# Twenty chunks of expert weights loaded ahead of the expert stage in place of sixteen

## The chip, the core and the metric

The kernel runs on one core of a Trainium2 chip. The metric is the device time of one execution in microseconds (us); lower is better. The core has TensorE (PE in the rows; its weight loads are PEld), VectorE (DVE), ScalarE (ACT), GpSimd (POOL) and SyncE (SP). SP computes nothing here: it issues most of the DMA transfers, one after the other in program order, and waits on semaphores between them. In the rows the issuing of a DMA has the engine name SPq or ACTq.

## What is computed

One step of a one-layer hybrid decoder for 256 prompt tokens and 64 sample tokens (320 in all, width 1024, float32): a token mixer of two branches (a chunked state-space scan with 16 heads, and an S5 scan), cross-attention into 256 memory tokens for each request, and a hierarchical mixture of experts: 4 groups of 8 experts, one group per token and the best two experts in it. The part that the change is about:

```python
def hier_moe(x, w_rg, b_rg, w_re, b_re, w_gate, w_up, w_down):   # x: 320 x 1024
    t = x.reshape(-1, D_MODEL)
    g_prob = jax.nn.softmax((t @ w_rg) + b_rg, axis=-1)
    g_idx = jnp.argmax(g_prob, axis=-1)
    ...
    comb = ((g_w * jax.nn.one_hot(g_idx, MOE_GROUPS))[:, :, None] * e_w[:, None, :])
    out = jnp.zeros_like(t)
    for g in range(MOE_GROUPS):                                  # 4 groups, 8 experts each
        hg = jax.nn.silu(jnp.einsum('td,edf->tef', t, w_gate[g])) * jnp.einsum('td,edf->tef', t, w_up[g])
        out = out + jnp.einsum('tef,efd->td', hg * comb[:, g, :, None], w_down[g])
    return out
...
h = h + memory_attention(rms_norm(h, norm_mem_q_g), mem_k, mem_v, w_mem_q, w_mem_o)
h = h + hier_moe(rms_norm(h, norm_ffn_g), ...)                   # then the final rms_norm
```

Each of the 32 experts has three matrices of 1024 x 512 in float32 (2 MiB each), so the expert weights are 192 MiB, and each is read once.

## The kernel before

**Stages.** The engines run programs of their own, written out by hand, with semaphores between them. First come the projections, the two scans and the gates; then the memory attention, whose sample part goes through the 8 requests one by one (SP fetches keys and values of 1 MiB each); then the output projection `o` in four parts of 256 columns and three blocks of tokens; then the router; then the expert stage, a loop over passes. A pass gives every expert up to 32 tokens; how many passes are needed is computed from the router's result, and these inputs need one.

**Units.** The 32 experts are handled in 8 quadruples (`NQ`), four experts side by side on TensorE (`EX = 4`, matmuls of 128x32 weights, which are the tokens, against 512 columns of expert weights). A quadruple `i` has six units: `U0` and `U1` (gate matrix, two halves), `U2` and `U3` (up matrix), `E0` and `E1` (down matrix). A unit needs four chunks of 1 MiB, one per expert. There are 48 units and 192 chunks; `ORDER` gives the units in time: U0 to U3 of quadruple 0, then for each next one its U0 to U3 followed by E0 and E1 of the quadruple before. TensorE's lines are L1888 (`gate_up`) and L1904 (`down`). Between the units stand side jobs (`phase_extras`): `X{i}.0` and `X{i}.1` gather the tokens of quadruple i with the selection `sel` (L1937), after which ScalarE and VectorE scale them into `xs` (L1161, L2641); `W{i}` turns the weights of the selected tokens (`selw`) into `wT`; `T{i}` transposes the hidden values, which VectorE writes in `hidden` (L2649); `S{i}.k` scatters the outputs back (L1963).

**Chunks and their places.** SP issues the 192 chunks in order (`load_chunk`, L588 and L590). The 16 places `raw[m % 16]` are regions of the two large tensors `ring` and `work`. The first 16 chunks go out while attention, the output projection and the router still run, and `left(m)` waits for the last reader of the place: chunk 0 for the sample attention of request 6 (`ob_full`), chunk 2 for request 7, chunk 5 for the last request, chunks 7 and 9 for the splitting of the first two parts of `w_mem_o`, chunks 11 and 13 for the third and fourth part of the output projection. From chunk 16 on SP waits at each multiple of four for the unit that held these four places (`unit_done`). The chunks of a unit count on a semaphore `raw_in`, one for each of four lanes; TensorE waits on it before the unit. The last unit's chunks are loaded in two halves (L588, L595).

**Around the start of the pass.** VectorE makes `sel` for quadruple 0, then (L2671 on) `weigh(0)` (L2628), `select(1)` (L2585) and `experts_in(0)` (L2641). TensorE starts with X0.0, with a matmul whose result is not used (`filler`, L1925) in its middle and another behind it, then U0. The router reads the transposed features `tT`, which eight `ft` jobs fill, and `lgT` is raised when the eighth logits matmul (L1799) has ended; ScalarE then copies the logits (L1133). While the router's small steps run, TensorE repeats matmuls whose result is not used (`busy`, L1836).

**The end.** After the last units VectorE adds up the output (L2663), multiplies the last rows by the final gain (`weighted`, L2669), and computes the variance (L2708) from the sums of squares that ScalarE made; then come the root, the scaling and the output DMAs.

## Time and profile before

| | |
|---|---|
| median of 3 runs | 1153.23 us |
| lowest and highest | 1151.77 and 1154.62 us |
| span of the profiled execution | 1153.6 us |
| TensorE matmul busy | 1001.8 us (87%) |
| VectorE busy | 460.6 us (40%) |
| ScalarE busy | 304.9 us (26%) |
| read from HBM | 286.76 MB |
| share of the main DMA queue | 65.5% of 16 engines |

The page shows one execution. Its busy times say how long an engine had instructions in it. The second part of the page cuts the span into 40 equal slices of 28.84 us; the row GB/s says what the DMA engines moved in each, and PEclk the clock that TensorE was granted, as a share of 2.4 GHz. In the rows of the timeline an instruction stands with its start, its duration, its engine and line, what it writes and reads, how many were merged (x4), and in brackets how long its engine had been idle and what ended that.

### The profile page before, as it was taken

What the parts mean: (1) busy time and instruction counts of PE and PEld (TensorE: products, weight loads), DVE (VectorE), ACT (ScalarE), POOL (GpSimd) and SP (SyncE); (2) the same over time, 40 slices, a digit from 0 to 9 for tenths busy, and PEclk for the clock granted to TensorE, in tenths of its full rate; (3) what the DMA queues carried; (4) which work ended last, traced back from release to release, by engine and by line L of the source; (5) the groups of instructions that cost most, each with busy time, mean ns of one, the idle gap of its engine ahead of it and who ended that gap; (6) DMA issues with size and microseconds to landing.
All of it is one profiled execution on the core that took longest, in us unless ns stands there. A gap on an engine that the chain in (4) does not pass through costs nothing.

```text
span 1153.6 us, 15983 instructions
## 1 busy us (share of the span) xinstructions
PE 1001.8 (87%) x6675; PEld 668.9 (58%) x6675; DVE 460.6 (40%) x787; ACT 304.9 (26%) x609; POOL 52.6 (5%) x76
## 2 busy tenths in 40 slices
PE   6999999999999999999898999867677877677565
PEld 4787567986679999999876954313131323232121
DVE  5999946204667554555455330010101010201014
ACT  3142123225436434544343331000000000000002
POOL 1604100010110000000000000000000000000000
PEclk9999999998999999999999999889788788887888
DMA  9482524012636284523677539999999999999994
GB/s 267 115 238 74 182 74 146 1 62 65 189 98 243 101 303 146 197 105 114 234 278 304 222 112 410 421 422 420 421 421 421 421 421 422 422 421 422 421 417 152
DMA packets 92435, 297.70 MB, mean 258 GB/s; under 512 B 21053, under 2 KB 31001, under 8 KB 68172
## 3 DMA queue, kind: packets, MB, share of 16 engines
q1 hardware_dynamic: 89812, 288.81, 65.5%
q0 software_dynamic: 2112, 7.28, 1.9%
q8 instruction: 54, 0.88, 0.3%
q10 hardware_dynamic: 440, 0.59, 0.2%
q14 instruction: 17, 0.14, 0.0%
HBM read 286.76 MB, written 9.90 MB: 257 GB/s over the span
## 4 chain that ended last, share of the span: by engine, by line
PE 40%; DMA 18%; SPq 13%; DVE 3%; issue 1%; ACT 1%; DVEq 0%; ACTq 0%
SPq L590 11%; DMA work<-in_w_exp_gate_dram 5%; DMA ring<-in_w_exp_down_dram 5%; PE bank L1607 5%; PE bank L1608 4%; PE bank L1609 4%; PE bank L1888 4%; DMA work<-in_w_exp_down_dram 3%; PE bank L1238 3%; DMA ring<-in_w_exp_gate_dram 2%; DMA ring<-in_w_exp_up_dram 2%; PE bank L1618 2%; PE bank L1620 2%; PE bank L1619 2%; PE bank L1937 2%; PE bank L1533 2%
## 5 line engine op out<-in xcount | busy, mean ns | idle before, releaser
L1888 PE MATMUL bank<-ring,work 128*32 128x512 f32 x768 | 139.7, 698 | 29.0 <-DMA work<-in_w_exp_gate_dram 14.9
L1888 PE MATMUL bank<-work 128*32 128x512 f32 x256 | 109.0, 690 | 22.2 <-DMA ring<-in_w_exp_gate_dram 15.3
L1253 PE MATMUL bank<-work,ring 128*128 128x320 f32 (+1 forms) x480 | 125.6, 420 | 0.0
L1607 PE MATMUL bank<-ops,usplit 128*128 128x320 f32 x368 | 114.2, 310 | 1.1 <-DVE usplit L2343 1.1
L1608 PE MATMUL bank<-ops,usplit 128*128 128x320 f32 x368 | 114.0, 310 | 0.0
L1609 PE MATMUL bank<-ops,usplit 128*128 128x320 f32 x368 | 113.9, 310 | 0.0
L1253 PEld LDWEIGHTS bank<-work,ring 128*128 128x128 f32 x480 | 90.2, 190 | 30.7 <-issue 1.0
L1904 PE MATMUL bank<-ring,work 128*32 128x512 f32 x384 | 86.4, 839 | 24.5 <-DMA ring<-in_w_exp_down_dram 13.1
L2343 DVE TENSOR_TENSOR usplit<-ring,usplit 128x2048 fp32r<-128x2048 f32 x32 | 73.3, 2291 | 62.3 <-ACT usplit L952 62.3
L1904 PE MATMUL bank<-work 128*32 128x512 f32 x128 | 63.6, 827 | 35.6 <-DMA ring<-in_w_exp_down_dram 35.6
L1888 PEld LDWEIGHTS bank<-ring,work 128*32 128x32 f32 x768 | 33.5, 126 | 76.1 <-issue 63.1
L952 ACT ACTIVATE usplit<-ring 128x2048 fp32r<-128x2048 f32 x32 | 61.4, 1920 | 51.9 <-PE bank L1609 36.7
L2641 DVE TENSOR_TENSOR work<-bank,g 128x512 f32<-128x512 f32 x8 | 5.5, 690 | 173.8 <-PE bank L1937 173.8
L1607 PEld LDWEIGHTS bank<-ops,usplit 128*128 128x128 f32 x368 | 69.2, 188 | 1.6 <-issue 1.5
L1937 PE MATMUL bank<-work 128*128 128x128 f32 (+1 forms) x384 | 69.4, 310 | 0.2 <-DVE work L2585 0.2
L1608 PEld LDWEIGHTS bank<-ops,usplit 128*128 128x128 f32 x368 | 69.1, 188 | 0.1
L1609 PEld LDWEIGHTS bank<-ops,usplit 128*128 128x128 f32 x368 | 69.2, 188 | 0.0
L1937 PEld LDWEIGHTS bank<-work 128*128 128x128 f32 (+1 forms) x384 | 53.0, 190 | 27.5 <-issue 14.0
L1888 PEld LDWEIGHTS bank<-work 128*32 128x32 f32 x256 | 23.2, 124 | 66.4 <-issue 58.2
L2656 DVE COPY work<-bank 128x512 f32<-128x512 f32 x8 | 5.5, 692 | 136.3 <-PE bank L1904 136.3
L1618 PE MATMUL bank<-usplit,ops 128*128 128x256 f32 (+1 forms) x192 | 54.6, 284 | 1.7 <-DVE ops L2348 1.7
L1620 PE MATMUL bank<-usplit,ops 128*128 128x256 f32 (+1 forms) x192 | 53.9, 281 | 0.0
(449 smaller groups left out, 1527.6 us busy)
## 6 DMA issues: line engine op xcount, KB each, us to landing
ring<-in_w_exp_up_dram SPq DMA_DIRECT2D x50, 1024.0 KB, 25.9
ring<-in_w_exp_gate_dram SPq DMA_DIRECT2D x46, 1024.0 KB, 26.0
ring<-in_w_exp_down_dram SPq DMA_DIRECT2D x45, 1024.0 KB, 26.0
ring<-in_w_in_dram SPq DMA_DIRECT2D x11, 2048.0 KB, 9.1
work<-in_w_exp_gate_dram SPq DMA_DIRECT2D x18, 1024.0 KB, 25.6
work<-in_w_exp_down_dram SPq DMA_DIRECT2D x15, 1024.0 KB, 25.6
work<-in_w_exp_up_dram SPq DMA_DIRECT2D x14, 1024.0 KB, 25.7
ring<-in_w_glu_dram SPq DMA_DIRECT2D x4, 2048.0 KB, 8.1
```

The costliest lines, as they stand in the source:

```text
L590: sp.dma_start(raw[m % RAW], src).then_inc(raw_in[m // EX % (RAW // EX)], 16)
L952: act.activation(uhi[u % 2], unit_raw(u), ACT.Copy).then_inc(s["whi"], 1)
L1253: ins = nc.tensor.matmul(b[:, 0:N], wv[:, k, P * (m % 4):P * (m % 4 + 1)], src[:, k, 0:N], start=(k == 0), stop=(k == KT - 1))
L1607: nc.tensor.matmul(b[:, 0:T], wh, hi_[:, k], start=(k == 0), stop=False)
L1608: nc.tensor.matmul(b[:, 0:T], wh, lo_[:, k], start=False, stop=False)
L1609: ins = nc.tensor.matmul(b[:, 0:T], wl, hi_[:, k], start=False, stop=(k == KT - 1))
L1618: nc.tensor.matmul(b[0:R, 0:256], th_, uhi[u % 2][:, k], start=(k == 0), stop=False)
L1620: ins = nc.tensor.matmul(b[0:R, 0:256], tl_, uhi[u % 2][:, k], start=False, stop=(k == KT - 1))
L1888: ins = nc.tensor.matmul(psum[part][ES * x:ES * (x + 1), :], xs[i % 2][:, kk, x], wt[x][:, k], start=(kk == 0), stop=(kk == KT - 1))
L1904: ins = nc.tensor.matmul(psum[2 + n_][ES * x:ES * (x + 1), :], hhT[:, j, x], wd[x][:, k, BLK * n_:BLK * (n_ + 1)], start=(j == 0), stop=(j ...
L1937: ins = nc.tensor.matmul(b[:, P * j:P * (j + 1)], tn[0:R, c, 4 * r_ + j], sel[i % 2][0:R, c].rearrange("p x n -> p (x n)"), start=(c == 0) ...
L2343: TT(ulo[u % 2], unit_raw(u), uhi[u % 2].bitcast(F32), ALU.subtract).then_inc(s["wlo"], 1)
```

## The change

The number of chunks that are loaded before the first unit is done goes from 16 to 20 (`AHEAD`). The four new places are:

- `early`: a new tensor of 2092 columns, out of which small tensors of the token mixer (`lpow`, `slp`, `lam`, `wdt`, `dtb`, `alog`, `cst`, `last3`, `dsm`) are now cut. Its chunk waits for `hl1`, a job of the state-space scan that is over long before. It takes part in the rotation for the rest of the pass.
- `xs` (columns 4096 to 6143 of `work`): the later home of `xs[1]`, `sel[1]` and `selw`. Chunk 6 goes there once the last request's attention is done.
- `ysb` (columns 6656 to 8703): the later home of the hidden values and the output sums. Chunk 14.
- `wT` (columns 18688 to 20735): the later home of `wT`. Chunk 15, when the router's logits are there (`lgT`).

The last three are used once, by the first twenty chunks; after that 17 places rotate, so that chunk m waits for the unit of chunk m - 17. The order in which the first twenty are issued is `BEGIN`. The semaphores `raw_in` go from four lanes to six.

So that the lent places stay untouched until their unit has read them, some work moves: `tT` goes to another part of `work`, `plc` and the scratch of the squares too; the matmuls `busy` read `h` in place of `tT`; VectorE does `experts_in(0)` first, then waits for unit U1 of quadruple 0, and only then does `weigh(0)` and `select(1)`, which write into the place of chunk 6; in quadruple 0 TensorE does X1.0 after U2 (before: after U1) and X1.1 after U3 (before: after U2). At the end of a pass VectorE waits for its own `weighted` results (`hg`) before it goes on to the variance.

```diff
-RAW = 16
+AHEAD = 20
+LANES = 6
+HOME = (["early", 0, 1, 2] + [3, 4, "xs", 5] + [6, 7, 8, 9] + [10, 11, "ysb", "wT"] + [12, 13, 14, 15])
+LENT = ("xs", "ysb", "wT")
+BEGIN = [0, 1, 2, 3, 4, 5, 6, 14, 7, 8, 9, 10, 11, 12, 13, 16, 17, 18, 19, 15]
+def places():
+    place, before_it = list(HOME), [None] * AHEAD
+    kept = [m for m in range(AHEAD) if HOME[m] not in LENT]
+    for m in range(AHEAD, NCH):
+        p = kept.pop(0)
+        place.append(place[p])
+        before_it.append(p)
+        kept.append(m)
+    return place, before_it
+PLACE, HELD_BY = places()
...
-        x["U1"] = [f"X{i + 1}.0"]
-        x["U2"] = [f"X{i + 1}.1"]
+        x["U2" if i == 0 else "U1"] = [f"X{i + 1}.0"]
+        x.setdefault("U3" if i == 0 else "U2", []).insert(0, f"X{i + 1}.1")
...
-        lpow = sb("lpow", [P, 2, Q + 1, NST])
+        early = sb("early", [P, 2092])
+        lpow = of_early(2, Q + 1, NST)
...
-        tT = w(3072, KT, T)
+        tT = [w(18296 + T * k, T) for k in range(KT - 1)] + [w(8704, T)]
...
-        plc = w(19680, NC, NG * NE)
+        plc = w(9088, NC, NG * NE)
...
+        home = dict(enumerate(raw)) | {"early": early[:, 0:CH], "xs": work[:, 4096:4096 + CH], "ysb": work[:, 6656:6656 + CH],
+                                       "wT": work[:, 18688:18688 + CH]}
...
-                if m == 0:
+                at = PLACE[m]
+                if at == "early":
+                    got(sp, "hl1")
+                elif at == 0:
                     sp.wait_ge(s["ob_full"], NB - 2)
-                elif m == 2:
+                elif at == 2:
                     sp.wait_ge(s["ob_full"], NB - 1)
-                elif m == 5:
+                elif at == "xs":
                     sp.wait_ge(s["ob_full"], NB)
...
+                elif at == "wT":
+                    sp.wait_ge(s["lgT"], 1)
...
-                for m in range(NCH):
+                for m in BEGIN:
                     left(m)
-                    if m >= RAW and m % EX == 0:
-                        sp.wait_ge(s["unit_done"], rr * NU + ((m - RAW) // EX + 1))
+                    load_chunk(m)
+                for m in range(AHEAD, NCH):
+                    u = HELD_BY[m] // EX
+                    if m == AHEAD or u > HELD_BY[m - 1] // EX:
+                        sp.wait_ge(s["unit_done"], rr * NU + (u + 1))
                     load_chunk(m)
...
-                    nc.tensor.matmul(psum[7][:, :], ones[:, :], tT[:, 0:2].rearrange("p k t -> p (k t)")[:, 0:BLK], start=True, stop=True)
+                    nc.tensor.matmul(psum[7][:, :], ones[:, :], h[:, 0, 0:BLK], start=True, stop=True)
...
+                experts_in(0)
+                unit("U", 0, 1)
                 weigh(0)
                 select(1)
-                experts_in(0)
...
                     dve.wait_ge(s[f"got{b}"], (rr + 1) * USES[b])
+                dve.wait_ge(s["hg"], rr * 2 + 2)
                 dve.sem_inc(s["pass_done"], 1)
```

SP's queue at the start of the pass, before: the names are the destination and the source tensor; the row with ISA is the wait for the first unit.

```order
L615 ISA
L590 DMA work<-in_w_exp_gate_dram 128x2048 x2
L590 DMA ring<-in_w_exp_gate_dram 128x2048 x2
L590 DMA work<-in_w_exp_gate_dram 128x2048
L590 DMA ring<-in_w_exp_gate_dram 128x2048 x3
L590 DMA ring<-in_w_exp_up_dram 128x2048 x7
L590 DMA work<-in_w_exp_up_dram 128x2048
L620 ISA
```

The same place in the changed kernel:

```order
L654 ISA
L624 DMA early<-in_w_exp_gate_dram 128x2048
L624 DMA work<-in_w_exp_gate_dram 128x2048 x2
L624 DMA ring<-in_w_exp_gate_dram 128x2048 x2
L624 DMA work<-in_w_exp_gate_dram 128x2048 x2
L624 DMA work<-in_w_exp_up_dram 128x2048
L624 DMA ring<-in_w_exp_gate_dram 128x2048
L624 DMA ring<-in_w_exp_up_dram 128x2048 x6
L624 DMA ring<-in_w_exp_gate_dram 128x2048 x3
L624 DMA work<-in_w_exp_gate_dram 128x2048
L624 DMA work<-in_w_exp_up_dram 128x2048
L662 ISA
```

Twenty transfers now stand ahead of the wait for the first unit, the four more being chunks 16 to 19 of quadruple 1's gate matrices, and the last issued is chunk 15.

TensorE between the units of quadruple 0, before, from the end of U1 to the start of U3 (L1888 is a unit's matmuls, 16 in all, and L1937 a side job X of 12):

```order
L1888 MATMUL bank<-ring,work 32x512 x3
L1930 REGISTER_ALU
L1937 MATMUL bank<-work 128x128 x12
L1888 MATMUL bank<-ring,work 32x512 x16
L1937 MATMUL bank<-work 128x128 x12
L1888 MATMUL bank<-ring,work 32x512 x3
```

The same place in the changed kernel, up to the first matmuls of the next quadruple's U0 (L1929 for L1888, L1978 for L1937; L1280 are the side jobs W0, of three, and T0, of four):

```order
L1929 MATMUL bank<-ring,work 32x512 x17
L1971 REGISTER_ALU
L1978 MATMUL bank<-work 128x128 x12
L1929 MATMUL bank<-ring,work 32x512 x2
...
L1978 MATMUL bank<-work 128x128 x12
L1280 MATMUL bank<-ident,work 128x128 x2
L1280 MATMUL bank<-ident,work 128x64
L1280 MATMUL bank<-ident,work 128x128 x4
L1929 MATMUL bank<-ring,work 32x512 x3
```

The last matmul of U1 and the sixteen of U2 are now one row; X1.0 stands behind them, and X1.1 between U3 and W0.

VectorE at the start of the pass, before, with the semaphores waited for:

```order
L2628 TENSOR_TENSOR work<-work,comb 128x384 [waits sel]
L2585 TENSOR_TENSOR work<-ranks,work 128x384
L2609 ISA
L2641 TENSOR_TENSOR work<-bank,g 128x512 [waits side4]
L2641 TENSOR_TENSOR work<-bank,g 128x512 [waits side7]
L2616 ISA [waits sil]
L2649 TENSOR_TENSOR work<-bank,work 128x512 [waits unit_done]
```

And in the changed kernel:

```order
L2682 TENSOR_TENSOR work<-bank,g 128x512 [waits side4]
L2657 ISA
L2668 ISA [waits unit_done]
L2669 TENSOR_TENSOR work<-work,comb 128x384 [waits sel]
L2626 TENSOR_TENSOR work<-ranks,work 128x384
L2682 TENSOR_TENSOR work<-bank,g 128x512 [waits side7]
L2657 ISA [waits sil]
L2690 TENSOR_TENSOR work<-bank,work 128x512 [waits unit_done]
```

The scaling of X0.0 (L2641, now L2682) has moved ahead of `weigh(0)` and `select(1)`, and a wait for a unit stands between them.

## Rows read from the trace of the kernel before

**Rows 1.** The page: span, and what the DMA engines moved in 40 slices.

```profile
span 1153.6 us, 15983 instructions
...
GB/s 267 115 238 74 182 74 146 1 62 65 189 98 243 101 303 146 197 105 114 234 278 304 222 112 410 421 422 420 421 421 421 421 421 422 422 421 422 421 417 152
```

**Rows 2.** DMA view from 760 to 1100 us.

```profile
DMA packets 19645, 143.20 MB, mean 421 GB/s; under 512 B 2177, under 2 KB 2177, under 8 KB 2177
```

**Rows 3.** Chain of work that ended last, in order of time: start, duration, what.

```profile
1124.22 11.20 DMA work<-in_w_exp_down_dram
```

**Rows 4.** Timeline of SP's queue: start, duration, line, transfer, count.

```profile
606.73 0.37 SPq L509 DMA_DIRECT2D ring<-in_cache_mem_v_dram  x1
613.73 0.82 SPq L590 DMA_DIRECT2D work<-in_w_exp_gate_dram  x2
...
625.90 1.28 SPq L590 DMA_DIRECT2D ring<-in_w_exp_gate_dram  x3
...
649.29 6.12 SPq L590 DMA_DIRECT2D ring<-in_w_exp_up_dram  x4
...
668.79 0.43 SPq L590 DMA_DIRECT2D work<-in_w_exp_up_dram  x1
...
691.08 0.80 SPq L590 DMA_DIRECT2D work<-in_w_exp_gate_dram  x2
```

**Rows 5.** Windows: stretch, length, engines' busy time, PEclk, DMA share, GB/s.

```profile
610.00:614.00 4.00, 3.94 (x49) 2.98 (x51) 2.12 (x5) 1.63 (x5) 0.00 (x0) 1.00 0.29 118
...
640.00:644.00 4.00, 4.00 (x37) 4.00 (x36) 1.51 (x3) 0.00 (x0) 0.00 (x0) 1.00 0.02 10
...
677.00:678.00 1.00, 1.00 (x4) 0.23 (x3) 0.70 (x4) 1.00 (x1) 0.00 (x0) 1.00 0.14 57
...
680.00:684.00 4.00, 4.00 (x16) 2.49 (x15) 2.48 (x11) 1.05 (x1) 0.00 (x0) 0.72 0.00 0
...
692.00:693.00 1.00, 1.00 (x7) 0.81 (x6) 0.00 (x0) 0.00 (x0) 0.00 (x0) 1.00 1.04 205
693.00:694.00 1.00, 1.00 (x8) 0.82 (x6) 0.00 (x0) 0.00 (x0) 0.00 (x0) 1.00 0.85 319
```

**Rows 6.** Timeline from the router's logits to the end of the first unit.

```profile
671.57 0.43 ACT L1133 ACTIVATE work<-bank 36x320 f32<-36x320 f32 x1 [0.84 <-PE bank L1799]
...
681.75 2.07 PE L1925 MATMUL bank<-work,ones 128*128 128x512 f32 x2
...
682.41 0.55 DVE L2585 TENSOR_TENSOR work<-ranks,work 128x384 f32<-128x384 f32 x1
...
686.33 1.13 PE L1925 MATMUL bank<-work,ones 128*128 128x512 f32 x2
...
686.43 0.69 DVE L2641 TENSOR_TENSOR work<-bank,g 128x512 f32<-128x512 f32 x1 [3.47 <-PE bank L1937]
...
687.38 0.62 PE L1888 MATMUL bank<-work 128*32 128x512 f32 x2
...
690.95 4.30 PE L1937 MATMUL bank<-work 128*128 128x128 f32 x24
```

**Rows 7.** Timeline of units U1 to U3 of quadruple 0 and their side jobs.

```profile
700.05 4.30 PE L1937 MATMUL bank<-work 128*128 128x128 f32 x24
...
704.28 3.64 PE L1888 MATMUL bank<-ring,work 128*32 128x512 f32 x32
...
715.78 1.05 DVE L2649 TENSOR_TENSOR work<-bank,work 128x512 f32<-128x512 f32 x1 [2.91 <-PE bank L1888]
...
716.98 0.63 PE L1238 MATMUL bank<-ident,work 128*128 128x128 f32 x4 [0.70 <-DVE work L2649]
717.54 0.62 PE L1888 MATMUL bank<-work 128*32 128x512 f32 x2
```

**Rows 8.** Timeline of VectorE at the end.

```profile
1142.55 0.68 DVE L2669 TENSOR_TENSOR work<-work,s5p 64x512 f32<-64x512 f32 x1
1143.15 0.14 DVE L2708 SCALAR_TENSOR_TENSOR var<-ssp,var 128x3 f32<-128x3 f32 x1
```

More of the change, by code:

```diff
@@ L50 @@
 NCH = EX * NU
-assert NCH % RAW == 0
 LASTU = NU - 1
+AHEAD = 20
[3 more added lines that the diff above has]
+BEGIN = [0, 1, 2, 3, 4, 5, 6, 14, 7, 8, 9, 10, 11, 12, 13, 16, 17, 18, 19, 15]
+assert len(HOME) == AHEAD and NU % LANES == 0 and sorted(BEGIN) == list(range(AHEAD))
+def places():
[8 more added lines that the diff above has]
+PLACE, HELD_BY = places()
 def phase_extras(i):
@@ L262, in layer, with of_early @@
         sel16 = sb("sel16", [P, 4, 2])
-        lpow = sb("lpow", [P, 2, Q + 1, NST])
-        slp = sb("slp", [P, 2, NST])
+        early = sb("early", [P, 2092])
+        early_at = [0]
+        def of_early(*dims):
+            n = 1
+            for d in dims:
+                n *= d
+            at = early_at[0]
+            early_at[0] += n
+            return view(early[:, at:at + n], dims)
+        lpow = of_early(2, Q + 1, NST)
+        slp = of_early(2, NST)
         vec = sb("vec", [P, 124])
-        lam = sb("lam", [P, 104])
+        lam = of_early(104)
         hglu = sb("hglu", [P, KT])
@@ L270, in layer @@
         s5p = sb("s5p", [P, 16, NST])
-        wdt = sb("wdt", [P, KT, HEADS])
+        wdt = of_early(KT, HEADS)
         wr = sb("wr", [P, KT, NG + NG * NE])
         rbias = sb("rbias", [P, NG + NG * NE])
-        dtb = sb("dtb", [P, HEADS])
-        alog = sb("alog", [P, HEADS])
-        cst = sb("cst", [P, CT, 3 * NB])
-        last3 = sb("last3", [P, CT, 27])
+        dtb = of_early(HEADS)
+        alog = of_early(HEADS)
+        cst = of_early(CT, 3 * NB)
+        last3 = of_early(CT, 27)
         ss = sb("ss", [P, 5])
@@ L295, in layer @@
         w_in_sem = [sem(f"w_slot{i}") for i in range(STAT_SLOTS)]
-        raw_in = [sem(f"raw_in{i}") for i in range(RAW // EX)]
+        raw_in = [sem(f"raw_in{i}") for i in range(LANES)]
         def bank(job):
@@ L391, in layer @@
         ytmp = w(23300, 192)
-        dsm = sb("dsm", [P, 12, NC, HEADS])
+        dsm = of_early(12, NC, HEADS)
         dtx, dte, dtl, dtm, dt_, dtA, csk, tot, wend, etot = (dsm[:, i] for i in range(10))
@@ L1115, in features @@
                 got(act, f"ft{k}")
-                emptied(act.activation(tT[:, k], bank(f"ft{k}")[:, 0:T], ACT.Copy), f"ft{k}")
+                emptied(act.activation(tT[k], bank(f"ft{k}")[:, 0:T], ACT.Copy), f"ft{k}")
             for i in range(3):
@@ L1798, in logits @@
                     pe.wait_ge(s["osb"], NB)
-                ins = nc.tensor.matmul(psum[6][0:NG + NG * NE, 0:T], wr[:, k], tT[:, k], start=(k == 0), stop=(k == KT - 1))
+                ins = nc.tensor.matmul(psum[6][0:NG + NG * NE, 0:T], wr[:, k], tT[k], start=(k == 0), stop=(k == KT - 1))
                 if k == KT - 1:
@@ L1873, in loaded @@
                 def loaded(u):
-                    n_ = RAW // EX
-                    pe.wait_ge(raw_in[u % n_], (rr * (NU // n_) + (u // n_ + 1)) * (16 * EX))
-                    return [raw[m % RAW] for m in range(EX * u, EX * u + EX)]
+                    pe.wait_ge(raw_in[u % LANES], (rr * (NU // LANES) + (u // LANES + 1)) * (16 * EX))
+                    return [home[PLACE[m]] for m in range(EX * u, EX * u + EX)]
                 def gate_up(i, j):
@@ L2513, in features @@
                 got(dve, f"ft{k}")
-                emptied(dve.tensor_copy(tT[:, k], bank(f"ft{k}")[:, 0:T]), f"ft{k}")
+                emptied(dve.tensor_copy(tT[k], bank(f"ft{k}")[:, 0:T]), f"ft{k}")
             dve.memset(rtl, 0.0)
```

17 lines of the change are left out of this document (9 added, 8 removed).

## The prediction

> **What bounds the kernel now.** I read the slices of the page first. From the 25th slice (692 us) to the 39th the DMA engines move some 421 GB/s in every slice, and in the four slices before they move 234 to 304, then 222 and 112 [rows 1]. The DMA view of the stretch from 760 to 1100 us gives the level exactly: 421 GB/s without a dip [rows 2]. So the expert stage is a stream of weights at one rate, and TensorE follows it. The chain of waits agrees: its last long piece is the wait of 11.20 us for w_exp_down, up to 1135.42, and behind it come only the last matmuls and the tail [rows 3]. A stage of this kind ends at (start of the gapless stream) + (bytes still to come) / (rate) + (tail). Whatever makes TensorE faster in it is worth nothing; what counts is when the stream starts and how much it still has to carry.
>
> Then I read where the stream starts. SP has issued the sixteenth chunk at 668.79 and can issue the next only at 691.08, when the first unit is done and its four places are free [rows 4]. The transfers end at about 677 (57 GB/s in 677 to 678), then nothing moves for some 15 us (0 GB/s from 680 to 684), and data flows again between 692 and 694 [rows 5]. The reader is to see an idle resource right ahead of the stretch in which it is the bound. The 15 us have room for six chunks, but no place to put them.
>
> **The change part by part.**
>
> *Four chunks out of the stream.* A chunk is 1 MiB, 1.0486 MB; at 421 GB/s [rows 2] it takes 2.49 us. When the first unit is done, 192 - 20 = 172 chunks are to come in place of 176. If all twenty have landed by then, the stream ends 4 x 2.49 = 9.96 us sooner. This term is the forecast; the rest is whether its conditions hold.
>
> *Do the four more transfers fit in idle DMA time?* Chunk 0 now goes to the early tensor, whose wait is long over, so it is issued right behind the last value load at 606.73, at about 607.1, and not at 613.73 [rows 4]. The DMA engines are 29% busy from 610 to 614 [rows 5]. The value load stands ahead of it in the queue and is for the last request, whose attention ends only at about 625.9, where SP's next wait ends [rows 4]; even a delay by one full chunk, 2.49 us, leaves that cover. The chunks for the xs and ysb places go out at 625.9 with the four others there, six in place of four, 5 us more of transfer. The old four have ended by 640 (10 GB/s from 640 to 644 [rows 5]), and SP's next issue is at 649.29 [rows 4]. So 5 us more end at about 645, in the hole. At about 668 SP issues three chunks as before (now 17, 18 and 19 where it was 13, 14 and 15), which end at about 677. The last one, chunk 15, waits for the logits; ScalarE copies those at 671.57 [rows 6], so it is queued by 671.7 and lands at 677 + 2.5 = 679.7 at the latest rate. All twenty are there 11 us before the first unit ends, and no step on the path waits for them. Cost of the four on the path: nothing, and 2.49 us for each that would not have landed in time.
>
> *The start of the first unit.* On VectorE the scaling of X0.0 moves ahead of weigh(0) and select(1). Before, these two instructions of 128x384 (0.55 us each, one at 682.41) ended by 683, and VectorE then sat idle for 3.47 us until X0.0 was there at 686.43 [rows 6]. So nothing was late by them and nothing is won. On TensorE the order up to the first unit is the same, with busy reading another tensor of the same shape. The first unit starts at 687.38 and ends at 690.95, 3.57 us, and SP issues 0.13 us later [rows 4, 6]. I take this as unchanged, 0 us. A bound below nothing: TensorE's clock is at 0.72 from 680 to 684 [rows 5], and the unused pair of matmuls takes 2.07 us there against 1.13 us at 686.33 [rows 6]. If the granted clock stayed at 2.4 GHz there, some 2 us would be won; if it came back later, about as much lost. Neither is in the change.
>
> *The new wait of VectorE for U1.* Behind it in its queue stand weigh(0), select(1), the scaling of X1.1 and hidden(0). TensorE needs select(1) for X1.0, which now comes after U2. In times of before: U1 ends at 700.05, the two instructions of 0.55 us are through by about 701.3, and U2 runs to 703.6, so X1.0 finds its selection. That is why X1.0 was moved, and U2 covers the wait. Without U2 the cost would be 1.2 us of TensorE, and none of the stream.
>
> *The next thing that is late: unit U0 of quadruple 1.* The stream must not run dry. After the first unit SP may issue chunks 20 to 23, after U1 24 to 26, after U2 27 to 30, after U3 31 and 32: 13 chunks, and the 14th waits for the fifth unit. Before, 16 chunks could be issued by then. So I compute both ends. The stream: 421 - 205 plus 421 - 319 are missing in the two windows from 692 to 694 [rows 5], which is 0.76 us, so it starts in effect at 692.76, 1.68 us behind SP's issue at 691.08. Thirteen chunks of 2.49 us keep it fed until 725.1. The unit: with 3.57 us for a unit [rows 6] and 4.23 us for a side job X (700.05 to 704.28 [rows 7]), U2 ends at 703.6, X1.0 at 707.85, U3 at 711.4, X1.1 at 715.65. The scaling of X1.1 takes 0.69 us and some 0.1 us of signal, to 716.45. hidden(0) then needs 1.20 us until T0 starts (715.78 to 716.98), and the unit starts 0.56 us after T0 (717.54) [rows 7]: 718.2, where it was 717.54. It ends at 721.8, SP issues at 721.9, and the data flows from 723.6. That is 1.5 us before the stream would run dry. Cost: nothing as computed; if this unit is late by more than 1.5 us, each further microsecond is paid in full. From there on the stream is fed in time, since each unit and its side jobs take at most 3.6 + 4.2 us and a unit's four chunks take 9.96 us.
>
> *Seventeen places in rotation.* Chunk m waits for the unit of m - 17 where it was m - 16. Since the stream has no dip in rows 2, a deeper rotation has nothing to give, 0 us.
>
> *The wait for hg at the end.* The trace of before does not show it. The second product starts at 1142.55 and takes 0.68 us, and the variance starts at 1143.15 without waiting for its end at 1143.23 [rows 8]. With the wait it starts a little after 1143.23. The bounds are 0.08 us (the rest of the product) and 0.7 us (a whole instruction of that size); I take 0.12 us, near the first, as only a signal comes on top. It is on the path: nothing covers it.
>
> *The sum.* -9.96 + 0.12 = -9.84 us. Against the profiled execution: 1153.6 - 9.8 = 1143.8 us. The median of the runs shown is 0.4 us below this span, so for the median 1153.23 - 9.84 = 1143.4 us.
>
> *A rule against a row.* The rate of the stream carries the whole term, and the trace shows 421 GB/s [rows 2]. The Trainium skill, "DMA: Bandwidth & Descriptors", section "Where 436 GB/s comes from", says that for transfers from HBM to SBUF the HBM side binds at about 358 GB/s. By an estimate from that page's figure a chunk would take 2.93 us and four would give 11.7 us. The row is measured in this very stretch, so the measurement decides, and that outcome gets no chance of its own.
>
> **The rivals.**
>
> *A. The stream runs dry for a while, or a chunk lands late.* The 14th chunk waits for a unit with 1.5 us to spare, and this margin is worked out from sums of a dozen short steps. If the chain from U3 to the next quadruple takes 3 to 5 us more than computed (a side job that waits for a semaphore I took as ready), 1.5 to 3.5 us go. If one of the four chunks does not land in time, 2.49 us go. Against it: the wait for the logits ends at 671.6 and leaves 11 us. Time: 1145 to 1148.5, say 1146.5 us.
>
> *B. The change does not do what it says.* If the DMA engines slowed down by what the chunks save, for instance because the stream writes places that TensorE reads at the same time more than before, the time would stay. It takes a rate of 421 x 172/176 = 411 GB/s over the stream. Against it: the stream holds 421 GB/s in fifteen slices through all sixteen places and all phases of TensorE. Time: 1153 us.
>
> *C. Slower: TensorE's clock.* TensorE falls to 1.2 GHz around 680, after the thin matmuls of the router, and is back before the first unit. If in the new order it came back only after quadruple 0, the first unit would take 3.6 us more, U1 to U3, the three X jobs and the fifth unit together some 27 us more (about what they take now, 691 to 721.8, less the waits), so the stream would start 3.6 us late and then be dry for 27 + 3.6 - 3.6 - 1.5 = 25.5 us: 3.6 + 25.5 - 9.8 = 19 us slower, 1172 us. It decides once its loss passes 9.8 us: beyond the first unit (3.6 us) and the 1.5 us to spare, when the low level lasts through 9.8 - 3.6 + 1.5, about 8 us of TensorE's work as it is timed now. Against it: the granted clock is 1.00 in 692 to 694 [rows 5], and the changed order puts U1 and U2 back to back, with fewer gaps and not more. The Trainium skill, "TensorE: Matmul & The Clock Gate", section "What's actually happening", says that the throttled clock is the default and activity releases it; by that rule, too, the new order is no worse.
>
> **How the numbers follow.** Forecast 1143.4 us with 0.80; within it the spread of a median (the three runs lie 1.5 us to either side) and the clock's 2 us around the first unit give 1141 to 1146. Rival A 0.12, rival B 0.04, rival C 0.02, and 0.02 for anything else that is slower. The range takes the forecast's own and half of rival A: 1140.8 to 1147.0. A measurement of this kernel tells about 0.3%, 3.5 us, from no change, so faster means below 1149.8: the forecast and rival A, 0.92. Same: rival B, 0.04. Slower: 0.04.
>
> **What would show it.** In the profile of the changed kernel: SP issues 20 chunks before its first wait for a unit, the last at about 671.7; the DMA engines are idle from about 680 to 692; the first unit still ends at about 691; the windows from 692 to 730 show 421 GB/s throughout (a dip near 724 would be rival A); the last pieces land some 10 us sooner, at about 1125.5; from there to the end of the span it takes 18.1 us, as before, plus 0.1. The forecast is wrong if the first unit ends more than 2 us later, or the stream's rate is not 421, or the windows around 724 dip.

## The result and the profile after

| | before | changed |
|---|---|---|
| median of the comparison (4 runs each) | 1153.42 us | 1145.51 us |
| lowest and highest | 1151.77 and 1154.62 us | 1144.06 and 1147.27 us |
| ratio with its 95% interval | | 0.9928 (0.9916 to 0.994) |
| span of the profiled execution | 1153.6 us | 1141.9 us |

The changed kernel is 7 to 10 us faster; the forecast was 1143.4 us, 9.84 us faster. In the comparisons of the experiments before has 54 runs with a mean of 1153.55 us. The changed kernel has nine runs, four here and five in e1, with a mean of 1145.18 us and a median of 1144.71 us. The means differ by 8.4 us, with a standard error of 0.4.

SP's queue in the profile after (the rows that answer to [rows 4]): start, duration, line, transfer, count.

```profile
606.81 0.37 SPq L542 DMA_DIRECT2D ring<-in_cache_mem_v_dram  x1
607.53 0.96 SPq L624 DMA_DIRECT2D early<-in_w_exp_gate_dram  x1
...
668.86 0.43 SPq L624 DMA_DIRECT2D work<-in_w_exp_gate_dram  x1
671.63 0.33 SPq L624 DMA_DIRECT2D work<-in_w_exp_up_dram  x1
689.54 0.33 SPq L624 DMA_DIRECT2D early<-in_w_exp_gate_dram  x1
...
698.64 0.33 SPq L624 DMA_DIRECT2D ring<-in_w_exp_up_dram  x1
```

Chunk 0 goes out at 607.53, chunk 15 at 671.63 (the forecast said 671.7), and the first refill at 689.54, where it was 691.08.

Windows of the profile after, to be held against [rows 5]: stretch, length, busy times of PE, PEld, DVE, ACT and POOL, granted clock, DMA share, GB/s.

```profile
677.00:678.00 1.00, 1.00 (x4) 0.21 (x3) 0.75 (x5) 1.00 (x1) 0.00 (x0) 1.00 0.99 418
678.00:680.00 2.00, 1.77 (x14) 1.62 (x15) 1.04 (x4) 1.95 (x5) 0.00 (x0) 1.00 0.81 340
680.00:684.00 4.00, 4.00 (x22) 2.80 (x21) 1.51 (x9) 1.11 (x1) 0.00 (x0) 1.00 0.02 10
...
698.00:702.00 4.00, 4.00 (x41) 1.07 (x33) 1.03 (x2) 0.60 (x1) 0.00 (x0) 1.00 1.01 424
...
720.00:724.00 4.00, 4.00 (x40) 1.32 (x32) 0.00 (x0) 0.34 (x1) 0.00 (x0) 1.00 1.02 424
```

The transfers that ended at 677 now run to 680, all twenty chunks are there, and the stream has no dip at 700 or at 724. The granted clock from 680 to 684 is 1.00, where it was 0.72 [rows 5].

The end in the profile after: first the last long piece of the chain of waits, then VectorE's timeline (compare [rows 3, 8]).

```profile
1112.25 11.07 DMA work<-in_w_exp_down_dram
```

```profile
1130.45 0.68 DVE L2710 TENSOR_TENSOR work<-work,s5p 64x512 f32<-64x512 f32 x1
1131.37 0.16 DVE L2751 SCALAR_TENSOR_TENSOR var<-ssp,var 128x3 f32<-128x3 f32 x1 [0.24 <-DVE work L2710]
```

The last weights are there at 1123.3, 12.1 us sooner. The variance starts 0.92 us behind the start of the product, where it was 0.60.

### The profile page after: what moved, and what is told of

Read it like the earlier page. It is cut to its first block, busy times and chain, and to the rows that moved or that the text cites. A ratio compares the mean times of both kernels' runs of the same rounds, so it can differ in the third digit from the quotient of the medians.

```text
span 1141.9 us, 15982 instructions
## 1 busy us (share of the span) xinstructions
PE 993.6 (87%) x6675; PEld 666.6 (58%) x6675; DVE 460.7 (40%) x787; ACT 304.6 (27%) x609; POOL 52.7 (5%) x76
## 4 chain that ended last, share of the span: by engine, by line
PE 36%; SPq 32%; DVE 3%; DMA 2%; issue 2%; ACT 1%; DVEq 0%; ACTq 0%
SPq L624 30%; PE bank L1649 5%; PE bank L1650 5%; PE bank L1651 5%; PE bank L1280 3%; PE bank L1929 2%; PE bank L1978 2%; PE bank L1660 2%; PE bank L1662 2%; PE bank L1661 2%; PE bank L1575 2%; SPq L622 1%; PE bank L1620 1%; DMA ring<-in_state_ssd_dram 1%; DMA work<-in_w_exp_down_dram 1%
## 5 line engine op out<-in xcount | busy, mean ns | idle before, releaser
L1929 PE MATMUL bank<-ring,work 128*32 128x512 f32 x704 | 130.9, 680 | 37.2 <-DMA ring<-in_w_exp_gate_dram 19.4
L1945 PE MATMUL bank<-ring,work 128*32 128x512 f32 x352 | 74.2, 818 | 40.7 <-DMA ring<-in_w_exp_down_dram 30.0
L1929 PE MATMUL bank<-work 128*32 128x512 f32 x256 | 85.7, 689 | 14.1 <-DMA work<-in_w_exp_up_dram 6.8
L1929 PEld LDWEIGHTS bank<-ring,work 128*32 128x32 f32 x704 | 32.0, 123 | 100.0 <-issue 80.3
L2682 DVE TENSOR_TENSOR work<-bank,g 128x512 f32<-128x512 f32 x8 | 5.5, 692 | 162.5 <-PE bank L1978 162.5
L1978 PE MATMUL bank<-work 128*128 128x128 f32 (+1 forms) x384 | 68.7, 308 | 0.2 <-DVE work L2626 0.2
L1978 PEld LDWEIGHTS bank<-work 128*128 128x128 f32 (+1 forms) x384 | 52.3, 188 | 27.2 <-issue 13.4
L1945 PEld LDWEIGHTS bank<-ring,work 128*32 128x32 f32 x352 | 17.6, 143 | 83.6 <-issue 54.8
L1945 PE MATMUL bank<-work 128*32 128x512 f32 x128 | 49.5, 820 | 10.2 <-DMA work<-in_w_exp_down_dram 10.2
```

What stands on the lines that cost most here:

```text
L1929: ins = nc.tensor.matmul(psum[part][ES * x:ES * (x + 1), :], xs[i % 2][:, kk, x], wt[x][:, k], start=(kk == 0), stop=(kk == KT - 1))
L1945: ins = nc.tensor.matmul(psum[2 + n_][ES * x:ES * (x + 1), :], hhT[:, j, x], wd[x][:, k, BLK * n_:BLK * (n_ + 1)], start=(j == 0), stop=(j ...
L1978: ins = nc.tensor.matmul(b[:, P * j:P * (j + 1)], tn[0:R, c, 4 * r_ + j], sel[i % 2][0:R, c].rearrange("p x n -> p (x n)"), start=(c == 0) ...
```

## Experiments

The sum had three parts that could be taken apart: what a chunk ahead is worth, what the moved work costs, and the wait for hg. A fourth question came from the traces: the span fell by 11.7 us but the time by 7.9, so the two profiles are not alike in something that the change doesn't touch, or the time outside the span has grown.

### The changed kernel again, sixteen places, seventeen places

**e1_again** is the changed kernel, unaltered.

> The changed kernel once more, unaltered, in five rounds, for a narrower ratio than the first one (0.9916 to 0.994, 7.0 to 9.7 us). The first comparison gave 7.9 us where the sum said 9.84. Theory 1 (the sum holds; the missing 1.9 us are the spread of the runs): the ratio comes out at about 0.9915, 9.8 us. Theory 2 (about 2 us are really lost somewhere): 0.993, 8 us. The profile also gives a second look at the granted clock between 680 and 684 us, which was 0.72 before and 1.00 after: chance would show both values in either kernel.

Measured: 1144.54 us (1144.37 to 1146.1, 5 runs), ratio 0.9933 (0.992 to 0.9945), 7.7 us. With the first comparison this favours theory 2: something like 1 to 2 us of the sum is missing.

**e2_moves_only** has the sixteen old places and all the moved work:

```diff
-AHEAD = 20
+AHEAD = 16
-HOME = (["early", 0, 1, 2] + [3, 4, "xs", 5] + [6, 7, 8, 9] + [10, 11, "ysb", "wT"] + [12, 13, 14, 15])
-BEGIN = [0, 1, 2, 3, 4, 5, 6, 14, 7, 8, 9, 10, 11, 12, 13, 16, 17, 18, 19, 15]
+HOME = list(range(16))
+BEGIN = list(range(16))
...
-                elif at == "xs":
+                elif at == 5:
```

> Sixteen chunks ahead in the sixteen old places, with everything else of the change (six lanes, tT and plc moved, VectorE's wait for U1 ahead of weigh(0) and select(1), X1.0 after U2 and X1.1 after U3, busy on h, the wait for hg). Theory 1: the moves cost 0.1 us (the wait for hg alone), 1153.5 us, ratio 1.000. Theory 2 (the moves eat part of the four chunks' gain): 1155.4 us, ratio 1.0017, and the difference shows at the start of the first unit or in the tail.

**e3_seventeen** adds the early tensor as a place:

```diff
-AHEAD = 20
+AHEAD = 17
+HOME = ["early"] + list(range(16))
+BEGIN = list(range(17))
```

> The same with the early tensor alone as a seventeenth place, no lent place. One chunk less in the stream. Theory 1: 2.49 us below e2_moves_only, 1151.0 us, ratio to before 0.9979. A rival, that a chunk loaded ahead is worth less than its time at the stream's rate (the stream starts later or runs slower by what it saves): 1.5 to 2 us below e2_moves_only.

Measured (ratios to before):

| kernel | chunks ahead | median | mean | ratio |
|---|---|---|---|---|
| e2_moves_only (11 runs) | 16 | 1154.88 us | 1154.76 us | 1.0014 (1.0004 to 1.0024) |
| e3_seventeen (12 runs) | 17 | 1152.71 us | 1152.60 us | 0.9993 (0.9984 to 1.0002) |
| changed, all nine runs | 20 | 1144.71 us | 1145.18 us | 0.9928 and 0.9933 |

So the first term holds. From 16 to 20 places the mean falls by 9.58 us, 2.40 us for a chunk; from 16 to 17 by 2.16 us (standard error 0.45), from 17 to 20 by 7.42, 2.47 each. The forecast's 2.49 stands inside all of these. The moves, priced at 0.12 us, cost 1.2 us on the mean (standard error 0.4). Most of the missing gain lies there. Theory 2 of e2 was right in size; in which places it is lost is the next question.

### Where the moves cost: the wait for hg, and the time outside the span

**e4_hg_behind** is the changed kernel with the wait elsewhere:

```diff
-                dve.wait_ge(s["hg"], rr * 2 + 2)
-                dve.sem_inc(s["pass_done"], 1)
                 dve.wait_ge(s["ss_fin"], rr * (2 * NC) + 2 * NC)
                 STT(out=var[:, 0:NC], in0=ssp[:, :, 1], ...).then_inc(s["var"], 1)
+                dve.wait_ge(s["hg"], rr * 2 + 2)
+                dve.sem_inc(s["pass_done"], 1)
                 dve.wait_ge(s["rs0"], rr + 5)
```

> The changed kernel with VectorE's wait for hg, and the signal that ends the pass, put behind the variance in place of ahead of it. The prediction's price for this wait is 0.12 us (bounds 0.08 and 0.7). From the start of the last matmuls to the end of the span it was 18.14 us before and is 18.53 after, 0.39 more. Theory 1: the wait is the 0.1 us of that, and the tail of this run is 18.4 us. Theory 2: the wait is all of it, tail 18.1 us and 0.4 us faster than e1_again.

Measured: 1143.81 us (5 runs), ratio 0.9927 (0.9914 to 0.9939); the mean is 1.0 us below e1_again's with a standard error of 0.6. VectorE's timeline of this run:

```profile
1129.14 0.68 DVE L2710 TENSOR_TENSOR work<-work,s5p 64x512 f32<-64x512 f32 x1
1129.74 0.15 DVE L2749 SCALAR_TENSOR_TENSOR var<-ssp,var 128x3 f32<-128x3 f32 x1
```

The variance is again 0.60 us behind the product, as in before. The wait costs 0.32 us, not 0.12: the variance starts 0.91 or 0.92 us behind the product in all six profiles that have the wait in its first place (after, e1, e2, e3, e8, e11), and 0.60 us in all that don't. The rest of the tail's 0.39 us is not from it: the last matmuls to the end of the span take 18.25 us here and 18.14 in before.

The list of runs gives the time and the span of each execution. The median of their difference, what lies outside the span, is 1.83 us for before (54 runs, none above 2.13), and 2.08 to 2.25 for everything with the change; the single runs of e5 and e6 below have 1.86 and 1.79. With the change a second thing appears that a median hides: 10 of the 60 runs have 2.7 to 3.2 us outside the span. So on the mean the difference is larger, 0.41 us for the changed kernel's nine runs (2.26 against 1.85) and 0.59 us for e2 (2.44). **e7_before_six_lanes** tests the one resource that all of these have more of, on the kernel before:

```diff
-        raw_in = [sem(f"raw_in{i}") for i in range(RAW // EX)]
+        raw_in = [sem(f"raw_in{i}") for i in range(6)]
...
-    sp.dma_start(raw[m % RAW], src).then_inc(raw_in[m // EX % (RAW // EX)], 16)
+    sp.dma_start(raw[m % RAW], src).then_inc(raw_in[m // EX % 6], 16)
...
-                    n_ = RAW // EX
+                    n_ = 6
```

> The kernel before with six semaphores raw_in in place of four. The time outside the profiled span is 1.83 us for before (median of 23 runs) and 2.14 to 2.25 for the kernels with the change, 0.3 us more. If the two more semaphores are the cause, this kernel has 2.1 us outside its span and a time of 1153.5 us; if the cause lies elsewhere (a longer program), 1.83 us and 1153.2 us.

Measured: 2.16 us outside the span (median of 10 runs), 0.33 us more than before, and nothing else changed. So six lanes lengthen this time. But the ten values are spread from 1.88 to 2.71 us, four of them at 1.88 to 1.93 as in before, and none of the 60 runs with the change is below 2.05; that the lanes explain all of the difference there is not shown. The time itself, 1154.22 us with a ratio of 0.9999 (0.9989 to 1.0009), can't tell 0.3 us from nothing. That the number of semaphores is the reason is not shown either: e10 below takes it back to that of before and keeps 2.10 us.

The 1.2 us of e2 are a difference of means, so what belongs beside them are the 0.59 us on the mean and the 0.32 us of the wait: 0.9 us. The 0.3 us that are left are within the standard error of 0.4.

### The clock ahead of the first unit

The two profiles differ in when the first unit starts. **e5_before_again** is before, unaltered; **e6_before_busy_h** has one operand changed:

```diff
-   nc.tensor.matmul(psum[7][:, :], ones[:, :], tT[:, 0:2].rearrange("p k t -> p (k t)")[:, 0:BLK], start=True, stop=True)
+   nc.tensor.matmul(psum[7][:, :], ones[:, :], h[:, 0, 0:BLK], start=True, stop=True)
```

> The kernel before, unaltered, for a second profile. The first profile of before had TensorE at a clock of 0.50 from 682 to 684 us and SP's first refill 23.13 us behind the issue of the three chunks near 668; all five profiles with the changed order have 1.00 there and 21.53 us. Theory 1 (chance of that one execution): 1.00 and 21.5 us here. Theory 2 (the change lifts the clock, since busy now reads h in place of tT): again near 0.5 and 23.1 us, and then the change has won 1.6 us that the sum did not contain.

> The kernel before, with the matmuls busy reading h in place of tT, nothing else. Theory 1 (chance): as e5_before_again. Theory 2: clock 1.00 between 680 and 684 and 21.5 us, in contrast to e5_before_again.

Two rows of SP's queue in e5, two of the three chunks near 668 and the first refill, and its window (columns as above):

```profile
667.89 0.80 SPq L590 DMA_DIRECT2D ring<-in_w_exp_up_dram  x2
...
689.43 0.80 SPq L590 DMA_DIRECT2D work<-in_w_exp_gate_dram  x2
```

```profile
680.00:684.00 4.00, 4.00 (x22) 2.80 (x21) 2.43 (x10) 0.99 (x1) 0.00 (x0) 1.00 0.00 0
```

And three windows of e6: the same stretch, one behind the first unit, and one with the stream's rate 11 us after its start.

```profile
680.00:684.00 4.00, 4.00 (x21) 2.80 (x22) 2.11 (x9) 0.61 (x1) 0.00 (x0) 1.00 0.00 0
...
696.00:698.00 2.00, 2.00 (x16) 0.65 (x12) 0.00 (x0) 0.00 (x0) 0.00 (x0) 0.50 1.03 434
...
700.00:702.00 2.00, 2.00 (x13) 1.52 (x13) 0.00 (x0) 0.45 (x1) 0.00 (x0) 1.00 0.93 270
```

Theory 1 holds: before has the full clock ahead of the first unit in one execution and half of it in another, so it needs no change of the kernel. SP's refill comes 21.54 us behind the three chunks near 668 in e5 and 23.13 in the first profile. e7, again the kernel before but for its lanes, has the low clock (0.66 from 684 to 688) and 23.15 us. The 11.7 us between the two spans therefore contain 1.6 us that come from this spell. What single profiles don't settle is whether it is as frequent in both orders: it stands ahead of the first unit in two of the four profiles with the old order, and in one of the ten with the new one (e12).

e6 shows a second thing. The low clock came behind the first unit there, U1 was late, and the stream fell to 270 GB/s between 700 and 702 and to 389 in the next two: 0.9 us lost. Four chunks last 9.95 us, and U1 ends 9.1 us behind the first unit (689.54 to 698.64 in the profile after). This point with 0.85 us to spare existed before the change, and the prediction did not look at it. Even at the full clock the two windows there dip a little in e1 and e3 (0.3 us each).

### The margin before the fifth unit

**e8_late_fifth** puts six unused matmuls ahead of the unit on which the 14th chunk waits:

```diff
                     if half == 0 and i:
                         pe.wait_ge(s[("sil", "hid")[part]], rr * NQ + i)
+                    if i == 1 and j == 0:
+                        for _ in range(6):
+                            filler()
```

> The changed kernel with six matmuls of no use (0.86 us each at the full clock, 5.2 us) ahead of the fifth unit, U0 of quadruple 1, on which the 14th chunk of the refill waits. The prediction says the stream has about 1.5 us to spare there (1.9 us in the profile after), so 3.3 to 3.7 us should be lost: 1148.2 us, and a dip of that length some 32 us behind the stream's start. The rival, that the DMA engines have chunks enough for longer: no loss, 1144.7 us.

Windows of e8:

```profile
720.00:722.00 2.00, 2.00 (x15) 0.60 (x17) 0.00 (x0) 0.00 (x0) 0.00 (x0) 1.00 0.99 410
722.00:724.00 2.00, 2.00 (x26) 0.55 (x20) 0.00 (x0) 0.00 (x0) 0.00 (x0) 1.00 0.57 238
724.00:726.00 2.00, 2.00 (x24) 0.62 (x20) 0.00 (x0) 0.00 (x0) 0.00 (x0) 1.00 0.30 49
726.00:728.00 2.00, 2.00 (x21) 0.45 (x13) 0.00 (x0) 0.00 (x0) 0.00 (x0) 1.00 0.84 291
```

The stream misses (183 + 372 + 130) x 2 / 421 = 3.25 us here, so 5.2 - 3.25 = 1.9 us were to spare at the full clock; the prediction had 1.5. The time is 1147.50 us, 2.8 us above the changed kernel's 1144.71 (ratio to before 0.9946, 0.9929 to 0.9962). The margin is real, it is that thin, and what exceeds it is paid: in the profile it is 3.3 us more from SP's refill to the end of the span (455.7 against 452.4 in after), and in the medians 2.8. So rival A's mechanism is there; at the full clock it costs nothing.

### Attempts at something better

**e9_u2_second**, on top of e4, makes U2 the second unit:

```diff
+def phases(i):
+    return ("U0", "U2", "U1", "U3", "E0", "E1") if i == 0 else PHASE
...
-        x["U2" if i == 0 else "U1"] = [f"X{i + 1}.0"]
+        x["U1"] = [f"X{i + 1}.0"]
...
-        x["U0"] = ["X0.1"]
+        x["U2"] = ["X0.1"]
...
-                    for c in PHASE:
+                    for c in phases(i):
...
-                unit("U", 0, 1)
+                unit("U", 0, 2)
```

> e4_hg_behind with U2 of quadruple 0 as the second unit (its chunks are then the second four, and X0.1 and U1 come behind it), X1.0 after U1, and VectorE waiting for U2. Theory: the stream is near dry not only before the fifth unit but after its first four chunks already: they last 9.95 us, and the second unit ends 9.1 us after the first, 0.85 us to spare, which a TensorE at the low clock between 692 and 698 uses up (1.2 us lost in e1_again, 0.9 in e2_moves_only, 1 in e6_before_busy_h; none in after). With U2 second the next chunks can be issued 3.6 us behind the first. Expected: no window below 375 GB/s 11 us behind the stream's start, and 0.4 us on the mean: 1143.4 us against 1143.8 of e4_hg_behind. The rival (these dips are noise of the transfers): the same dips, 1143.8 us.

The 1.2 us that this expectation names for e1_again came from the length of the whole stream; its windows from 700 to 704 (381 and 406 GB/s) show only 0.3 us there. The rest lies in late arrivals, which the section on the prediction describes. Measured: 1143.34 us (5 runs), ratio 0.9919 (0.9905 to 0.9934), mean 1143.96 against e4's 1143.89. Its windows:

```profile
688.00:690.00 2.00, 2.00 (x27) 0.53 (x18) 0.00 (x0) 0.00 (x0) 0.00 (x0) 1.00 0.23 37
690.00:692.00 2.00, 2.00 (x24) 0.51 (x16) 0.00 (x0) 0.00 (x0) 0.00 (x0) 1.00 0.77 221
692.00:694.00 2.00, 2.00 (x15) 1.40 (x11) 1.03 (x2) 0.00 (x0) 0.00 (x0) 1.00 1.01 389
694.00:696.00 2.00, 2.00 (x13) 1.57 (x12) 0.00 (x0) 0.00 (x0) 0.00 (x0) 1.00 0.96 385
...
698.00:700.00 2.00, 2.00 (x24) 0.58 (x20) 0.00 (x0) 1.02 (x1) 0.00 (x0) 1.00 1.00 418
700.00:702.00 2.00, 2.00 (x21) 0.74 (x13) 0.00 (x0) 0.52 (x1) 0.00 (x0) 1.00 1.00 422
```

There is no dip 11 us behind the start, as expected. But the start is softer. By 696 us the stream has moved (37 + 221 + 389 + 385) x 2 = 2064 KB, as if it had begun at 691.1 at the full rate, 2.16 us behind SP's issue at 688.94; in e4 the same reckoning gives 1.74 us. SP's second and third issue take longer:

```profile
689.31 2.42 SPq L628 DMA_DIRECT2D work<-in_w_exp_gate_dram  x2
```

In after and in e4 these two take 0.91 us. Why is open. The profile of e4 has no dip that U2 could have removed, so a gain of this placement is not shown, and the means don't tell e9 from e4.

**e10_two_semaphores_less** puts two lanes on semaphores that are done:

```diff
-        raw_in = [sem(f"raw_in{i}") for i in range(LANES)]
+        raw_in = [sem(f"raw_in{i}") for i in range(LANES - STAT_SLOTS)] + w_in_sem
+        raw_base = [0] * (LANES - STAT_SLOTS) + [16 * len(BLOCKS[i::STAT_SLOTS]) for i in range(STAT_SLOTS)]
...
-                    pe.wait_ge(raw_in[u % LANES], (rr * (NU // LANES) + (u // LANES + 1)) * (16 * EX))
+                    pe.wait_ge(raw_in[u % LANES], (rr * (NU // LANES) + (u // LANES + 1)) * (16 * EX) + raw_base[u % LANES])
```

> e9_u2_second with the fifth and sixth lane of raw_in on the two semaphores w_slot of the projection weights, whose last wait is long over, so two semaphores less. e7_before_six_lanes had 2.16 us outside the span against 1.84 of before. Expected: 1.84 us outside the span, and 0.3 us faster than e9_u2_second. This is the version meant to beat both kernels: 1143.1 us.

Measured: 1144.38 us (1141.6 to 1146.38), mean 1144.13, ratio 0.9914 (0.9899 to 0.9929), 2.10 us outside the span. The expectation of 1.84 us failed, so it is not the count of semaphores alone; nor is this the version that beats the others. This profile has the low clock in two places, near 700 and near 720, and shows the thin margin at the fifth unit used up in the kernel's own course (1.1 us missing from 724 to 728):

```profile
700.00:704.00 4.00, 4.00 (x32) 0.87 (x24) 0.00 (x0) 0.31 (x1) 0.00 (x0) 0.76 1.01 426
720.00:722.00 2.00, 2.00 (x15) 0.45 (x9) 0.00 (x0) 0.00 (x0) 0.00 (x0) 0.50 1.04 434
...
724.00:726.00 2.00, 2.00 (x24) 0.65 (x20) 0.00 (x0) 0.00 (x0) 0.00 (x0) 1.00 0.83 229
726.00:728.00 2.00, 2.00 (x17) 0.79 (x10) 0.00 (x0) 0.56 (x1) 0.00 (x0) 1.00 0.93 373
```

**e11_no_middle_filler** is the changed kernel without the unused matmul inside X0.0, and **e12_both** has this and e4's edit:

```diff
-                        if i == 0 and r_ == 0 and j == 2:
-                            filler()
```

> The changed kernel without the unused matmul in the middle of X0.0. It takes 0.97 us of TensorE ahead of the first unit at the full clock, and more at the low one. The stream's start is on the path, so each microsecond there should count in full: SP's first refill 20.56 us behind the three chunks near 667 in place of 21.53, 1143.9 us. The rival: the clock falls for want of this matmul, the first unit takes up to 3.6 us more, and the time is 1145 to 1148 us.

> e4_hg_behind and e11_no_middle_filler in one: VectorE's wait for hg behind the variance, and no unused matmul in the middle of X0.0. The first is worth 0.32 us by the tail of the profiles (variance 0.60 us behind the last product in place of 0.92), the second 0.86 us by SP's first refill (20.67 us behind the three chunks near 667 in place of 21.53). If both add up: 1.2 us below the changed kernel's 1144.9 (median of its nine runs), 1143.7 us on the mean. If the clock falls more often without that matmul, the gain of the second goes, and this kernel is at e4_hg_behind's 1143.9 us or above, with a window of low clock between 684 and 704.

(The median of the nine runs is 1144.71, not the 1144.9 of the last text.) Measured: e11 1144.21 us (1142.45 to 1148.83), mean 1144.92, ratio 0.9928 (0.9904 to 0.9953); e12 1143.47 us (1142.43 to 1147.69), mean 1144.02, ratio 0.9916 (0.9902 to 0.9929). In e11's profile SP's refill comes 20.67 us behind the chunks near 667 and not 21.53: the 0.86 us are won. Its clock is low from 692 to 696 and from 716 to 720, and the stream misses 0.7 us near 700 and 0.8 near 723. e12's profile is that of its slowest run, and its windows show why:

```profile
680.00:684.00 4.00, 4.00 (x17) 3.08 (x16) 1.49 (x9) 1.09 (x1) 0.00 (x0) 0.61 0.01 6
684.00:690.00 6.00, 6.00 (x22) 2.51 (x25) 0.69 (x1) 0.00 (x0) 0.00 (x0) 0.50 0.00 0
```

The clock is low for some 10 us, through X0.0 and the first unit, and the refill comes 25.37 us behind, 4.7 more than in e11. The other four runs of e12 took 1142.4 to 1143.6 us. e4, e9, e10, e11 and e12 all have means of 1143.9 to 1144.9 us against the changed kernel's 1145.2, and are not told apart from each other. The wait behind the variance is the one edit that a profile shows to be worth something (0.32 us) at no risk; taking the matmul away wins 0.86 us in the one profile that has the full clock there, and both of its kernels had one run some 4 us above the rest.

## Why the prediction was right, and where it was off

- **The bound.** Right. The stream keeps 421 GB/s after as before (the slices of the page after show 420 to 422 from the 26th to the 38th), and the whole gain came from its start and its bytes.
- **2.49 us for each chunk.** Right: 2.40 per chunk from 16 to 20 places in e2 and the changed kernel, 2.16 to 2.47 for the parts.
- **Four transfers in idle time.** Right: in the profile after the last is issued at 671.63, the DMA engines are idle from about 680, and the unit ends at 689.4. The issue of the early chunk at 607.53 delayed nobody: the next wait of SP ends at 613.75, where it was 613.73 [rows 4].
- **VectorE's new order.** Right in that it costs nothing: SP's first refill comes 21.53 or 21.54 us behind the chunks near 668 in eight of the profiles with the new order, as in before's second profile; the other two have the unused matmul removed (20.67) or that and the low clock as well (25.37).
- **The fifth unit's margin.** Right in kind and nearly in size: 1.5 us forecast, 1.9 by e8. Its consequence was seen too mildly. It isn't always enough when the clock falls, which e10 and e11 show with 1.1 and 0.8 us lost.
- **The wait for hg, 0.12 us.** Mis-sized; it is 0.32 us. The bounds held it (0.08 and 0.7), but the value put only 0.04 us on top of the rest of the instruction, where the row after shows 0.24 us of idle.
- **A term that was missing.** The time outside the span was taken as unchanged; it grew by 0.33 us on the median and 0.41 on the mean, and e7 ties at least a part of that to the six lanes.
- **A place that was not looked at.** The first four chunks leave only 0.85 us for U1. Before the change it was so too; the prediction computed the end of thirteen chunks and not the end of four.
- **The profile against the median.** The forecast set the median of the times 0.4 us below the span of the profile. That is a coincidence of two unlike executions: the profiled one took its span plus some 1.8 us, well above the median, and the clock had fallen ahead of its first unit. The forecast of 1143.4 us is not touched by this, since it subtracts from the median, but the difference between the two profiles is.

With the measured terms, all on the mean, the sum is -9.96 + 0.32 + 0.41 = -9.2 us; measured are 8.4, with a standard error of 0.4. So of the 1.4 us between the forecast and the measured difference, 0.6 are the two terms that were missing or too small, and the last 0.9 us are not settled. The dips near 700 us (0.9 us in e2, 0.3 in e1 and e3, none in after and e4) are one candidate, but e6 shows such a dip without the moves as well, and single profiles don't tell how often each kernel has them.

The traces show a second candidate. A chunk counts sixteen arrivals on its semaphore, and a unit can start only with the last of its 64. In after and e1, the same kernel at the full clock, the arrivals of the 46th unit of 48 lie 407.6 and 407.8 us behind SP's first refill on the mean, but the last of them 413.2 and 414.7 us. In before and e5, again one kernel, it is 417.5 and 417.6 us on the mean, and 423.8 and 422.9 for the last. So two executions of one kernel differ by 0.9 to 1.5 us in the slowest part of the transfers, which the rate in GB/s does not show. From the refill to the end of the span it is 462.5 us in before and 461.7 in e5, 452.4 in after and 453.9 in e1: the difference lies between 7.8 and 10.1 us, according to the pair that is compared. Whether the change alters these late arrivals on the mean, no run here tells.

Rival B is excluded by the rate in the pages. Rival C's low clock is real, but it came in before as well, and ahead of the first unit it cost 1.6 to 4.7 us, never 19: it did not last through the quadruple in any of the profiles.

The figure of the Trainium skill, "DMA: Bandwidth & Descriptors", section "Where 436 GB/s comes from", some 358 GB/s for transfers from HBM, does not bind here, as the prediction judged: the stream holds 421 GB/s, and the gain per chunk (2.40 us) speaks against the 2.93 us that would follow from it by an estimate.

## What to carry to other kernels

Where a stage is one stream at a fixed rate, look for idle time right ahead of it and price every place that can be freed by its bytes over that rate; it holds to a few per cent. Then list every point at which the stream waits for a consumer, the first ones above all, and write down the time to spare at each: a margin below what a spell of the low clock costs (here 1.6 us and more) is lost in some executions. Before believing the difference of two spans, see whether a clock or another chance event differs ahead of the bound stage or in it. And when terms are added up against a difference of means, take every term as a mean: here the time outside the span had a second level in one run of six, which its median hid.

## What the runs showed of the hardware

- Two executions of the same kernel can differ in the clock that TensorE is granted over the same instructions: 0.72 and 1.00 from 680 to 684 us. Between 680 and 704 us the low spell lies ahead of the first unit in three profiles (before, e7, e12), behind it in e2, e6, e10 and e11, and in neither place in after, e1, e3, e4, e5, e8 and e9. Ahead of the first unit TensorE had just done the router's thin matmuls; behind it TensorE had just been waiting. Neither is enough by itself: from 692 to 696 TensorE is busy for 2.77 of 4.00 us both in e2, where the clock falls to 0.60 from 694, and in after, where it stays at 1.00. In e12 it lasted 10 us, into the dense matmuls of the first unit (0.50 from 682 to 690).
- Waiting for one's own result of 64x512 on VectorE put the next, independent instruction 0.92 us behind the start of the first in place of 0.60.
- Of the sixteen arrivals that each transfer counts, the last can drift against the mean within one execution and back. In e1 against after the mean arrival of every unit from the seventh on is within 0.2 us; the last one is 1.4 to 1.6 us later for the units 16 to 24 and 40 to 48, and within 0.2 us for the others.
- Six semaphores in turn for the chunks' arrival, in place of four, lengthened the time outside the profiled span from 1.83 to 2.16 us on the median with the same instructions and transfers (e7). Reusing two older semaphores did not bring it back (2.10 us in e10); the cause is open.
- SP's issue of the same two transfers took 0.91 us in after and e4 and 2.42 us in the kernels with U2 second (e9, and 2.43 us in e10); in e9 the stream started 0.4 us later behind the first issue. Also open.
